# Forgetting attention of a two-block transformer: values of pair n-2 and scores of pair n side by side, turns three slots behind their scores

## What is computed

```python
z = h @ w_in
q, k, v = (16 heads of 64 each); zf = z[..., 3 * hd:]
logf = jax.nn.log_sigmoid(zf + b_f)
c = jnp.cumsum(logf, axis=-1)                 # over the tokens, per head
sc = einsum("bhqd,bhkd->bhqk", q, k) / sqrt(dh) + c_t - c_s
sc = jnp.where(tpos >= key_pos, sc, NEG)
p = jax.nn.softmax(sc, axis=-1)
o = einsum("bhqk,bhkd->bhqd", p, v)
return o @ w_out
```

## Time and profile before

| | us |
|---|---|
| median of 3 runs | 1610.25 (1610.21 to 1610.54) |
| span of the profiled execution | 1607.8 |
| PE busy | 1592.8 (99%) |
| DVE busy | 1092.2 (68%) |
| ACT busy | 920.2 (57%) |
| POOL busy | 53.9 (3%) |

### The profile page before, as it was taken

How to read it: one execution, slowest core, us unless ns; L and a number is a source line. 1 busy time by engine, 2 the same in 40 slices (tenths; PEclk the granted TensorE clock), 3 DMA queues, 4 the chain that set the end, 5 groups by cost and what they waited for, 6 DMA issues and landing times.

```text
span 1607.8 us, 23572 instructions
## 1 busy us (share of the span) xinstructions
PE 1592.8 (99%) x9247; PEld 1356.0 (84%) x9247; DVE 1092.2 (68%) x1759; ACT 920.2 (57%) x1553; POOL 53.9 (3%) x96
## 2 busy tenths in 40 slices
PE   8999999999999999999999999999999999999998
PEld 6887888889888888888887788888888889888887
DVE  5877776778667777665677566567666667775665
ACT  5756754567665555644576564456454474674544
POOL 4000000000030000000002100000000000000000
PEclk9999999999999999999999999999999999999999
DMA  8444666546355555656555465654665654456562
GB/s 293 136 145 153 232 224 192 188 145 197 94 196 187 192 175 177 212 175 203 185 153 182 118 208 183 196 185 158 221 185 185 193 189 148 124 173 204 187 185 77
DMA packets 212225, 287.67 MB, mean 179 GB/s; under 512 B 11052, under 2 KB 180334, under 8 KB 212116
## 3 DMA queue, kind: packets, MB, share of 16 engines
q1 hardware_dynamic: 208500, 280.00, 55.0%
q0 software_dynamic: 3616, 6.17, 1.4%
HBM read 284.47 MB, written 3.87 MB: 179 GB/s over the span
## 4 chain that ended last, share of the span: by engine, by line
PE 96%; DMA 1%; DVE 1%; ACT 1%; SPq 0%; issue 0%; POOL 0%; DVEq 0%
PE two L2191 89%; PE two L2268 1%; PE two L2450 1%; PE two L2437 1%; PE two L2460 1%; DMA x_tok<-in_x 1%; DVE w_lo L1462 1%; PE two L2575 0%; PE two L2823 0%; PE two L2254 0%; DMA vals<-u_dram 0%; PE two L2463 0%; ACT p_sb L1033 0%; DMA u_dram<-aux 0%; PE two L2431 0%
## 5 line engine op out<-in xcount | busy, mean ns | idle before, releaser
L2191 PE MATMUL two<-act_parts,w_hi 128*128 128x512 f32 (+1 forms) x2784 | 802.0, 353 | 0.0
L1462 DVE TENSOR_TENSOR w_lo<-raw,w_hi 128x1024 fp32r<-128x1024 f32 (+1 forms) x520 | 612.9, 1220 | 114.8 <-ACT w_hi L844 114.3
L2191 PE MATMUL two<-act_parts,w_lo 128*128 128x256 f32 x2256 | 634.9, 281 | 0.0
L2191 PEld LDWEIGHTS two<-act_parts,w_hi 128*128 128x128 f32 x2784 | 486.9, 188 | 82.0 <-issue 6.2
L844 ACT CAST w_hi<-raw 128x1024 fp32r<-128x1024 f32 (+1 forms) x520 | 516.3, 1048 | 6.1 <-DMA raw<-in_ffn_w_up 4.5
L2191 PEld LDWEIGHTS two<-act_parts,w_lo 128*128 128x128 f32 x2256 | 425.5, 189 | 2.1
L2191 PE MATMUL two<-w_hi,act_parts 128*128 128x512 f32 (+2 forms) x832 | 249.8, 380 | 2.4 <-ACT w_hi L844 2.3
L973 ACT COPY p_sb<-two 128x512 f32<-128x512 f32 x108 | 62.5, 579 | 247.0 <-PE two L2191 247.0
L2191 PE MATMUL two<-w_hi,hid_even 128*128 128x512 f32 x576 | 187.8, 393 | 0.0
L2191 PEld LDWEIGHTS two<-w_hi,act_parts 128*128 128x128 f32 x832 | 151.5, 189 | 33.4 <-issue 3.0
L1590 DVE TENSOR_TENSOR pt_sb<-two,p_sb 128x512 f32<-128x512 f32 x54 | 37.3, 691 | 198.5 <-ACT p_sb L973 198.5
(11 more groups left out here) (317 smaller groups left out, 1199.5 us busy)
## 6 DMA issues: line engine op xcount, KB each, us to landing
raw<-in_ffn_w_up SPq DMA_DIRECT2D x160, 512.0 KB, 4.0
raw<-in_ffn_w_down SPq DMA_DIRECT2D x132, 512.0 KB, 3.5
raw<-in_ffn_w_gate SPq DMA_DIRECT2D x80, 512.0 KB, 3.8
raw<-in_a_w_in SPq DMA_DIRECT2D x24, 512.0 KB, 4.6
raw<-in_fox_w_in SPq DMA_DIRECT2D x20, 512.0 KB, 3.7
raw<-in_ffn_w_up SPq DMA_DIRECT2D x32, 256.0 KB, 3.6
raw<-in_w_kv SPq DMA_DIRECT2D x12, 512.0 KB, 3.6
raw<-in_mem_w_kv SPq DMA_DIRECT2D x8, 512.0 KB, 10.7
```

Of the source, the lines that this page charges most:

```text
L1462: nc.vector.tensor_tensor(w_lo[:, r, 0:n], raw[:, r, 0:n], w_hi[:, r, 0:n], ALU.subtract).then_inc(lo_done, 1)
L2191: return nc.tensor.matmul(dst, a, w, start=start, stop=stop, skip_group_check=True)
```

## The change

It reorders the stage on PE, ACT and DVE; no instruction is added or taken away, and the order of SP and POOL is untouched. PE's order becomes

```diff
 # ACT
-            for m in range(4):
+            for m in range(3):
                 t = fox_slots(m, 0)
                 splits(t + 8)
-                if m == 3:
-                    o_hi("fox", 5)
+                if m:
+                    o_hi("fox", 2 * m - 2)
                 exps("fox", 2 * m)
-                if m in (1, 2):
+                if m:
+                    pt_copy("fox", 2 * m - 1)
+                splits(t + 9)
+                if m:
                     o_hi("fox", 2 * m - 1)
-                splits(t + 9)
                 exps("fox", 2 * m + 1)
                 pt_copy("fox", 2 * m)
-                splits(t + (11 if m == 3 else 10))
-                pt_copy("fox", 2 * m + 1)
-                o_hi("fox", 2 * m)
+                splits(t + 10)
+            t = fox_slots(3, 0)
+            splits(t + 7)
+            o_hi("fox", 4)
+            pt_copy("fox", 5)
+            splits(t + 8)
+            exps("fox", 6)
+            o_hi("fox", 5)
+            splits(t + 9)
+            exps("fox", 7)
+            pt_copy("fox", 6)
+            splits(t + 10)
+            pt_copy("fox", 7)
+            splits(t + 11)
+            o_hi("fox", 6)
+            o_hi("fox", 7)
             splits(455)
-            o_hi("fox", 7)
             splits(457)
 # DVE
-            for m in range(4):
+            for m in range(3):
                 t = fox_slots(m, 0)
-                if m:
-                    o_lo("fox", 2 * m - 2)
                 splits(t + 8)
                 scores("fox", 2 * m)
                 if m:
+                    o_lo("fox", 2 * m - 2)
+                take_pair(m + 1, 0)
+                probs("fox", 2 * m)
+                splits(t + 9)
+                scores("fox", 2 * m + 1)
+                if m:
                     o_lo("fox", 2 * m - 1)
-                if m < 3:
-                    take_pair(m + 1, 0)
-                probs("fox", 2 * m)
-                scores("fox", 2 * m + 1)
-                splits(t + 9)
+                take_pair(m + 1, 1)
                 probs("fox", 2 * m + 1)
-                splits(t + (11 if m == 3 else 10))
-                if m < 3:
-                    take_pair(m + 1, 1)
+                splits(t + 10)
+            t = fox_slots(3, 0)
+            splits(t + 7)
+            o_lo("fox", 4)
+            splits(t + 8)
+            scores("fox", 6)
+            probs("fox", 6)
+            o_lo("fox", 5)
+            splits(t + 9)
+            scores("fox", 7)
+            splits(t + 10)
+            probs("fox", 7)
+            splits(t + 11)
             o_lo("fox", 6)
+            o_lo("fox", 7)
             splits(454)
-            o_lo("fox", 7)
             splits(457)
 # PE
                 fox_part(m, 0, 0)
                 if m > 1:
-                    values("fox", 2 * m - 3)
+                    values("fox", 2 * m - 4)
                 fox_scores(2 * m - 2)
                 fox_part(m, 0, 1)
+                if m > 1:
+                    turns("fox", 2 * m - 3)
+                fox_part(m, 1, 0)
+                if m > 1:
+                    values("fox", 2 * m - 3)
                 fox_scores(2 * m - 1)
-                fox_part(m, 1, 0)
+                fox_part(m, 1, 1)
                 turns("fox", 2 * m - 2)
-                fox_part(m, 1, 1)
-                if m < 3:
-                    turns("fox", 2 * m - 1)
-                    values("fox", 2 * m - 2)
-            values("fox", 4)
-            turns("fox", 5)
             pe.wait_ge(h_olo, PAIR0["fox"] + 4)
             fox_out(0, 0)
+            values("fox", 4)
+            fox_scores(6)
             fox_out(1, 0)
-            fox_scores(6)
-            values("fox", 5)
+            turns("fox", 5)
             pe.wait_ge(h_olo, PAIR0["fox"] + 5)
             fox_out(0, 1)
+            values("fox", 5)
             fox_out(1, 1)
+            fox_out(2, 0)
             fox_scores(7)
-            for b in range(NTB):
-                fox_out(2, b)
+            fox_out(2, 1)
+            fox_out(3, 0)
             turns("fox", 6)
-            for b in range(NTB):
-                fox_out(3, b)
+            fox_out(3, 1)
+            fox_out(4, 0)
             turns("fox", 7)
+            fox_out(4, 1)
             values("fox", 6)
-            fox_out(4, 0)
             values("fox", 7)
             fox_out(5, 0)
+            fox_out(5, 1)
             out_end("fox", pair_ready("fox", 0), 0)
-            for i in range(4, NCH - 2):
-                fox_out(i, 1)
             out_end("fox", pair_ready("fox", 0), 1)
```

## The result

The changed kernel takes 1616.77 us (median of 5, 1616.37 to 1616.92) against 1610.54 (1610.21 to 1611.18) before: a ratio of 1.0038, 95% interval 1.0027 to 1.0048, or 6.2 us more. The forecast was 1614.9 with a range up to 1616.6: the direction holds, the size is past the upper end.

A forecast was written before the change was run, and what follows sets the result against it. The prediction took the stage as a queue of PE work without a hole; -0.6 (joins) + 2.8 + 1.6 + 0.8 (three new PE waits) = +4.6 us on the median 1610.25 gave 1614.9, range 1612.4 to 1616.6.

The forecast's parts named there:

- PE's own work: PE's matmul order in the stage: three more joins of values (V) with scores (S), 0.19 us each, 0.6 us less.
- the 0.3 that the prediction worked out from it: Joins of V and S: by the skill's drain rule a join saves one of two mode changes, 0.3 instead of 0.6 us.
- Scores 7: Scores of pair 7 (S7): PE waits 2.8 us, as the chain from turns 5 takes 8.70 against PE's 5.93; bounds 2.3 to 3.2.
- Turns 7: Turns of pair 7 (T7): PE waits 1.6 us for probs 7, held by slot 452's rounding and subtraction; bounds 1.2 to 2.0.
- End of the stage: Transposes of x: PE waits 0.8 us, with four slots rounded on ACT instead of two; bounds 0.3 to 1.4.
- The clock: PE's granted clock in the stage, 1.00 before: the sum had no term for a fall.
- rival (c): Between scores 7 and turns 7: PE's holes bring the clock down to half pace, 5.8 us on top, 1621; chance 0.05.
- Rival (a): Stage's waits partly covered: scores 7 waits, turns 7 and the norm find their work done, 1612.4 to 1613.3; chance 0.10.
- Rival (b): Whole stage: nothing waits and the joins alone count, 1609.7 us, not slower; chance 0.06.

The follow-up runs named there:

- the sixth experiment: Changed kernel with roundings of slots 450 and 452 early on ACT, 453 to 455 ahead too, end of block 0 ahead of out(5,1): 1609.05 us, ratio 0.9995.
- the second: Changed kernel with the roundings of slots 450 and 452 moved ahead of the copies of pairs 5 and 6 on ACT: 1610.51 us, ratio 1.0001.
- the first experiment: Changed kernel with the rounding of slot 450 moved ahead of the upper part of pair 4 and the copy of pair 5 on ACT: 1612.44 us, ratio 1.0013.

## Why the prediction was wrong in size

- **PE's own work**, -0.6: -0.64 measured, with all waits out of the way. One term of it can be read by itself. From S2 to S4 both kernels do the same work, after the change with one join of V and S more, and without the V behind T. After, and then S4 before:

```profile
1355.50 0.44 PE L2455 MATMUL two<-rowf,pick 64*128 64x384 f32 x2
...
1372.29 0.44 PE L2455 MATMUL two<-rowf,pick 64*128 64x384 f32 x2
```

```profile
1373.04 0.44 PE L2431 MATMUL two<-rowf,pick 64*128 64x384 f32 x2
```

  16.79 after and 16.96 before (from 1356.08): 0.17 for a join, forecast 0.19. Two of them leave 0.30 for V6 beside V7 and all else, where 0.19 stood. But 0.80 is not V's bare length, as the prediction has it: V6 to V7, of one form, take 0.70, V to a weight matmul 0.80 (1390.11 to 1390.91 in the trace of before), V to S 0.80. So leaving V for S costs 0.10, as leaving it for the weights does. The Trainium skill, TensorEngine Tiling (Array Packing), section Key Properties, says that a change of the tiling mode drains TensorE; these 0.10 agree with it, where the prediction read the trace the other way. What did not come true is the 0.3 that the prediction worked out from it: a join saves 0.17, and not half of 0.19.
- **Scores 7**, +2.8: 2.79 idle, and S0 to S7 2.86 longer than in the sixth experiment. Right, with its chain: moving the rounding of 450 takes the wait away, and moving T5 shortens it by what T5 gains.
- **Turns 7**, +1.6: 1.46 idle, T6 to T7 5.05 as forecast, and T6 to V6 1.69 longer than in the sixth experiment. Right; the rounding of 452 alone makes it.
- **End of the stage**, +0.8: 0.31 idle ahead of the transposes of x and 0.29 within them, which take 1.32 instead of 1.03; start to start V6 to the transposes of block 1 take 15.25 against 14.53 in the sixth experiment, 0.72. Right. The four slots of rounding from 1413.47 on took 3.91 us, where 4.00 stood in the sum.
- **The clock**, 0 in the sum: this is the step that failed. The sum carried the work behind S7 at the pace of rows 7, and rival (c), PE's holes bring the clock down, got a chance of 0.05 because no row of the stage had a hole to show it. It did fall: 0.50 for some 3.4 us, +1.57. From start to start the stage takes 86.73 us after (1340.15 to 1426.88) and 80.53 before, and the 6.20 between them is the whole of what was measured: 2.86 + 1.69 + 0.72 + 1.57 - 0.64 = 6.20. Without the clock it is 4.63, where the forecast had 4.6. That the top of the forecast's bounds, +6.3, comes near the +6.2 is luck: it has all three waits at their longest, which they were not, and nothing for the clock.
- **Rival (c)** named the mechanism but was priced at 5.8 instead of 1.57. It took half pace until T7. The clock was back by 1404, still ahead of T6; and its working let T7's wait take up part of the loss, whereas that wait is counted from T6 and stayed 1.46. The Trainium skill, TensorE: Matmul & The Clock Gate, Part 1, says that an idle TensorE is gated down to 1.2 GHz; the trace agrees with 0.50. It adds, of the start of a kernel, that the same kernel shows a different number of slow matmuls in different runs, as the hardware's watch runs free of the program; the two executions with a hole of 1.81 differ in this way too, but no run here shows the reason.
- **Rival (a)** did not occur. **Rival (b)** is what the sixth experiment made: roundings 450 and 452 ahead of the copies, the end mended, and only the joins left; the second did so but for the end.

The versions without the waits are not measurably faster than the kernel before (0.9995, 0.9986 to 1.0004). What stays open: from how short a hole on the clock may fall, and in which share of executions. All the holes behind which it fell stood ahead of scores 7; whether what follows a hole matters, no run tells. A wait of 1.8 us at an earlier stage, for the transfer of values in the profile of the first experiment, did not bring it.

## What to carry to other kernels

Where PE works without a hole, moving a step of PE's moves every chain that begins at it: count from its start along each engine's written order, and look for work that nobody needs yet (here a rounding of a weight slot) standing between a hand-over and the step that PE waits for; moving two such roundings won nearly all of it. Count a new hole on PE twice: its own length, and the slower pace that may follow, here 1.5 to 1.6 us behind holes of 2.8 and 2.9. And when one kernel's times lie in two groups, take the profile more than once, and measure the stage in it from start to start, before explaining the median.

## What was not expected of the hardware

The clock fell behind idle times of 2.79, 2.80 and 2.94 us in their profiles, did not behind 1.43, 1.46 and 2.12 in theirs, and behind 1.81 it did once and did not twice. It fell not at the hole but after work had resumed (from about 1400.5 on, S7 having started at 1398.92, in the changed kernel; at 1397.0, S7 having started at 1396.81, in the first of the two executions with 1.81), and was back after 3 to 4 us. With matmuls that only add zeros in the hole it stayed at 1.00 in each of the three profiles (three, six and twelve of them).
